# Expert rounds of 96 and 64 slots in turn, constants in two loads, and the filling of the row buffer moved

## The reference

```python
def moe_ffn(h, router, w_gu, w_down):
    logits = (h @ router).astype(jnp.float32)
    top_v, top_i = lax.top_k(logits, TOP_K)          # TOP_K = 2 of N_EXPERTS = 8
    w = jax.nn.softmax(top_v, axis=-1)
    combine = jnp.sum(jax.nn.one_hot(top_i, N_EXPERTS, dtype=jnp.float32) * w[..., None], axis=-2)
    gu = jnp.einsum('btd,edf->btef', h, w_gu)        # w_gu: 8 x 1024 x 2816
    g, u = jnp.split(gu, 2, axis=-1)
    act = jax.nn.silu(g) * u * combine[..., None].astype(h.dtype)
    return jnp.einsum('btef,efd->btd', act, w_down)  # w_down: 8 x 1408 x 1024
```

## Time and profile before

| | us |
|---|---|
| median of 3 runs (2498.81 to 2507.88) | 2501.84 |
| the profiled execution's own time | 2506.24 |
| its span in the profile | 2504.4 |
| PE busy | 2345.0 (94%) |
| the seven 96-slot rounds of layer 1, from 808.09 | 7 x 52.53 |
| the seven of layer 3, from 2047.40 | 7 x 52.53 |

### The profile page before, as it was taken

How to read it: one execution, slowest core, us unless ns; L and a number is a source line. 1 busy time by engine, 2 the same in 40 slices (tenths; PEclk the granted TensorE clock), 3 DMA queues, 4 the chain that set the end, 5 groups by cost and what they waited for, 6 DMA issues and landing times.

```text
span 2504.4 us, 47903 instructions
## 1 busy us (share of the span) xinstructions
PE 2345.0 (94%) x21465; PEld 1684.2 (67%) x21465; DVE 478.7 (19%) x1359; ACT 401.4 (16%) x843; POOL 67.2 (3%) x111
## 2 busy tenths in 40 slices
PE   5999998999999999999799899999989899999997
PEld 3776667888888544555476588888878675455454
DVE  1234332000113100000021410003345340000001
ACT  1133223000101000000112310002243310000000
POOL 5000000000000000000000000000000000000000
PEclk8999999999998999999999899999999989999998
DMA  9867886653363898999465695323420079899971
GB/s 329 286 235 270 306 314 199 188 156 102 101 202 126 315 345 309 338 346 330 166 194 193 213 278 164 113 67 104 156 78 11 12 279 332 312 344 348 345 264 42
DMA packets 356876, 551.67 MB, mean 220 GB/s; under 512 B 11393, under 2 KB 311937, under 8 KB 344241
## 3 DMA queue, kind: packets, MB, share of 16 engines
q1 hardware_dynamic: 344208, 525.30, 60.6%
q0 software_dynamic: 5840, 17.72, 2.6%
q10 hardware_dynamic: 6688, 6.57, 0.8%
HBM read 537.24 MB, written 16.37 MB: 221 GB/s over the span
## 4 chain that ended last, share of the span: by engine, by line
PE 88%; DVE 4%; ACT 3%; DMA 3%; issue 1%; ACTq 0%; POOL 0%; SPq 0%; POOLq 0%; DVEq 0%
PE ps L632 86%; ACT ring L1334 1%; DMA ring<-in_dn_w_in 1%; ACT work L1334 1%; DMA ring<-in_ada_w 1%; PE ps L1129 1%; DVE ring L1866 0%; DVE ring L1848 0%; DMA work<-y_rows,work 0%; DVE ring L1871 0%; DVE work L1708 0%; DVE ring L1856 0%; PE ps L1022 0%; DMA y_rows<-work 0%; DMA work<-in_x_sample 0%
## 5 line engine op out<-in xcount | busy, mean ns | idle before, releaser
L632 PE MATMUL ps<-ring,work 128*32 128x256 f32 (+5 forms) x9576 | 783.6, 429 | 35.7 <-ACT work L1334 27.9
L632 PE MATMUL ps<-hT,ring 128*128 128x256 f32 x3200 | 711.8, 381 | 5.2 <-DMA ring<-in_dn_w_in 2.8
L632 PEld LDWEIGHTS ps<-hT,ring 128*128 128x128 f32 x3200 | 607.3, 191 | 114.5 <-issue 12.1
L632 PEld LDWEIGHTS ps<-ring,work 128*32 128x32 f32 (+2 forms) x9576 | 394.9, 114 | 402.8 <-issue 242.8
L1334 ACT ACTIVATE work<-ps 128x256 f32<-128x256 f32 (+4 forms) x268 | 110.3, 428 | 1438.7 <-PE ps L632 1243.5
L632 PE MATMUL ps<-work,ring 128*128 128x256 f32 (+1 forms) x1344 | 291.0, 376 | 10.7 <-DVE work L1933 6.2
L632 PEld LDWEIGHTS ps<-work,ring 128*128 128x128 f32 (+1 forms) x1344 | 243.9, 189 | 48.1 <-DVE work L1933 8.4
L632 PE MATMUL ps<-ring 64*64 64x64 f32 (+1 forms) x4192 | 182.4, 229 | 18.1 <-ACT ring L1334 7.2
L632 PEld LDWEIGHTS ps<-ring 64*64 64x64 f32 x4192 | 160.0, 138 | 57.0 <-ACT ring L1334 24.2
L1334 ACT ACTIVATE ring<-ps 128x512 f32<-128x512 f32 (+3 forms) x208 | 101.7, 492 | 342.4 <-PE ps L632 331.3
L632 PE MATMUL ps<-ring,csil 128*2 128x512 f32 x768 | 99.9, 608 | 10.9 <-DMA ring<-in_ada_w 10.7
(11 more groups left out here) (252 smaller groups left out, 985.6 us busy)
## 6 DMA issues: line engine op xcount, KB each, us to landing
ring<-in_moe_w_gu SPq DMA_DIRECT2D x96, 1536.0 KB, 10.0
ring<-in_ada_w SPq DMA_DIRECT2D x96, 1024.0 KB, 7.3
ring<-in_moe_w_down SPq DMA_DIRECT2D x48, 1536.0 KB, 11.5
ring<-in_ff_w_gu SPq DMA_DIRECT2D x88, 512.0 KB, 6.0
ring<-in_dn_w_in SPq DMA_DIRECT2D x32, 1024.0 KB, 5.5
ring<-in_moe_w_gu SPq DMA_DIRECT2D x32, 1024.0 KB, 5.5
ring<-in_ff_w_down SPq DMA_DIRECT2D x44, 512.0 KB, 7.2
ring<-in_moe_w_down SPq DMA_DIRECT2D x32, 512.0 KB, 6.3
```

Source lines behind the costliest of these rows:

```text
L632: return pe.matmul(out, lhsT, rhs, start=start, stop=stop, **kw)
```

## The change

The seven rounds of up to 96 slots become rounds of 96 and 64 in turn. DVE ranks experts 1 to 7 by their picks: the three smallest go to rounds 1, 3 and 5 with 64 slots, the next three to rounds 2, 4 and 6 with 96, the largest to round 7 with 128. Expert 0 stays in round 0 with 96. In a 64-slot round the four column groups hold the 64 tokens twice, against two different parts of the weights. The constants are loaded in two parts, the second in front of the first panel. The filling of `y_rows` goes behind DeltaNet's state stores, and the position table waits for the first panel to be used.

```diff
-CAP, BLK, GW, DW = 96, 32, 384, 256
+CAP, SMALL_CAP, BLK, GW, DW = 96, 64, 32, 384, 256
+ROUND_CAP = [CAP, SMALL_CAP, CAP, SMALL_CAP, CAP, SMALL_CAP, CAP] + [P] * (1 + EXTRA + 1)
...
         @block.sync
-            sp.dma_start(cst[:], a["consts"]).then_inc(consts_in, 16)
+            sp.dma_start(cst[:, 0:C_TF], a["consts"][:, 0:C_TF]).then_inc(consts_in, 16)
...
                 for name, i in sequence(l):
+                    if (l, name, i) == (0, "in", 0):
+                        sp.dma_start(cst[:, C_TF:NCONST], a["consts"][:, C_TF:NCONST]).then_inc(consts_in, 16)
...
                                 sp.wait_ge(moe["p_gu"], (done[0] + r) * 6 + GU_FREE[j])
+                                if j in (GATE_D, UP_D):
+                                    sp.wait_ge(moe["p_dn"], (done[0] + r) * 4 + 1)
...
         @block.gpsimd
-            for x in range(RND):
-                r0 = CAP if x < NARROW else 0
-                po.dma_start(y_rows[P * x + r0:P * (x + 1), :], a["x_prompt"][0, r0:P]).then_inc(filled, 16)
...
+            po.wait_ge(unit_done, PLAN.first[0]["in"][0] + 1)
             po.memset(rpb_sb[0:48, :], 0.0).then_inc(o_z, 1)
...
             dn_states(0)
+            for x in range(RND):
+                r0 = ROUND_CAP[x] if x < NARROW else 0
+                po.dma_start(y_rows[P * x + r0:P * (x + 1), :], a["x_prompt"][0, r0:P]).then_inc(filled, 16)
...
         @block.tensor
             def deltanet(l):
                 i = DN_LAYERS.index(l)
+                pe.wait_ge(consts_in, 32)
...
+                def columns_small(q, pieces, bank, done):
+                    for j, _ in pieces:
+                        landed(q, j)
+                    for k in range(KC):
+                        for x, (j, width) in enumerate(pieces):
+                            for b in range(2):
+                                t = 2 * x + b
+                                ins = mm(ps[BLK * t:BLK * (t + 1), bank, 0:width], xg[:, k, BLK * b:BLK * (b + 1)],
+                                         weights(j, width)[:, k, :], k == 0, k == KC - 1)
+                    ins.then_inc(moe["p_gu"], done)
...
+                def down_small(q, s):
+                    pe.wait_ge(moe["a_at"], q * 3 + (1 + 2 * s))
...
+                    for c in (range(6, 11) if s else range(6)):
+                        w, n = down_rows(c), c - 6 * s
+                        for b in range(2):
+                            at = P * (n % 3) + 64 * (n // 3) + BLK * b
+                            for x in range(2):
+                                t = 2 * x + b
+                                ins = mm(ps[BLK * t:BLK * (t + 1), 4 + x, :], ma_T[:, s, at:at + BLK],
+                                         w[:, 512 * x:512 * x + 512], c == 0, c == 10, skip_group_check=True)
+                        if c in (2, 4, 7, 10):
+                            ins.then_inc(moe["p_dn"], 1)
+
+                def small(q):
+                    pe.wait_ge(moe["a_xg"], q + (i + 1))
+                    pe.wait_ge(moe["d_xg"], q + (i + 1))
+                    columns_small(q, ((GATE[0], GW), (GATE[1], GW)), PG[0], 1)
+                    columns_small(q, ((UP[0], GW), (UP[1], GW)), PU[0], 3)
+                    columns_small(q, ((GATE[2], GW), (GATE_D, DW)), PG[1], 1)
+                    columns_small(q, ((UP[2], GW), (UP_D, DW)), PU[1], 1)
+                    turn_small(q, 0)
+                    down_small(q, 0)
+                    pe.wait_ge(moe["d_act"], q * 3 + 3)
+                    pe.wait_ge(moe["d_g"], q + (i + 2))
+                    gather(0)
+                    gather(1)
+                    turn_small(q, 1)
+                    down_small(q, 1)
...
                 body(q0, True)
-                with pe.Fori(1, NARROW) as r:
-                    body(q0 + r, False)
+                with pe.Fori(1, NARROW, 2) as r:
+                    small(q0 + r)
+                    body(q0 + r + 1, False)
...
         @block.vector
             def overflow(l):
                 link(stt(taken[:, 0:NE], count, float(NE), es, ALU.mult, ALU.subtract))
-                link(dve.tensor_reduce(top_e, taken[:, 1:NE], AX.X, ALU.max))
-                link(ts(is_top, taken[:, 0:NE], top_e, None, ALU.is_equal))
...
+                link(tt(before_e[:, 0, :, 1:NE], taken[:, 0:NE, None].to_broadcast([P, NE, NARROW]),
+                        taken[:, None, 1:NE].to_broadcast([P, NE, NARROW]), ALU.is_gt))
+                link(dve.tensor_reduce(rank, before_e[:, 0, :, 1:NE], AX.X, ALU.add))
+                ts(high[:, 0], rank, 2.5, None, ALU.is_gt)
+                ts(high[:, 1], rank, 5.5, None, ALU.is_gt)
+                link(ts(where[:, 0:NE], rank, 2.0, 1.0, ALU.mult, ALU.add))
+                link(stt(where[:, 0:NE], high[:, 0], -5.0, where[:, 0:NE], ALU.mult, ALU.add))
+                link(tt(where[:, 0:NE], where[:, 0:NE], high[:, 1], ALU.subtract))
...
```

More of the change, by code:

```diff
@@ new lines, in turn_small @@
+                def turn_small(q, s):
+                    pe.wait_ge(moe["d_act"], q * 3 + (1 + 2 * s))
+                    if s == 1:
+                        pe.wait_ge(moe["a_at"], q * 3 + 1)
+                    for c in range(2 if s else 3):
+                        ins = pe.transpose(ps[:, 6, c * P:(c + 1) * P], ma_s[:, s, c * P:(c + 1) * P], ident)
+                    if s == 1:
+                        ins = pe.transpose(ps[:, 6, 2 * P:2 * P + 64], ma_s[0:64, s, 2 * P:3 * P], ident[0:64, 0:64])
+                    ins.then_inc(moe["p_tr"], 1 + s)
@@ new lines, in down_small @@
+                def down_small(q, s):
+                    pe.wait_ge(moe["a_at"], q * 3 + (1 + 2 * s))
+                    if s == 0:
+                        pe.wait_ge(moe["a_y"], q)
+                        pe.wait_ge(moe["d_y"], q)
+                        for j in (8, 9):
+                            landed(q, j)
+                    else:
+                        landed(q, 10)
+                    for c in (range(6, 11) if s else range(6)):
[8 more added lines that the diff above has]
+                            ins.then_inc(moe["p_dn"], 1)
@@ L1555, in store, with output_small, store_small, small @@
                             .then_inc(moe["y_out"], 16)
+                def output_small(q):
+                    act.wait_ge(moe["p_dn"], q * 4 + 4)
+                    act.wait_ge(moe["y_out"], q * 64 + 64)
+                    f(y_m[0:64, :], ps[0:64, 4, :], ACT.Copy).then_inc(moe["a_y"], 1)
+                def store_small(q, r):
+                    act.wait_ge(moe["a_y"], q + 1)
+                    act.wait_ge(moe["d_y"], q + 1)
+                    for x in range(4):
+                        act.dma_start(y_rows[bass.ds(r * P, 64), QUARTER * x:QUARTER * (x + 1)],
+                                      y_m[64 * (x // 2):64 * (x // 2) + 64, QUARTER * (x % 2):QUARTER * (x % 2 + 1)]) \
+                            .then_inc(moe["y_out"], 16)
+                def small(r):
+                    q = q0 + r
+                    output(q - 1)
+                    act.wait_ge(moe["p_gu"], q * 6 + 1)
+                    act.wait_ge(moe["d_act"], q * 3)
+                    f(mg_s, ps[:, PG[0], 0:GW], ACT.Silu).then_inc(moe["a_silu"], 1)
+                    store(q - 1, r - 1)
+                    act.wait_ge(moe["p_gu"], q * 6 + 5)
+                    act.wait_ge(moe["d_act"], q * 3 + 1)
+                    f(mg_s[0:64, DW:GW], ps[0:64, PG[1], DW:GW], ACT.Silu)
+                    f(mg_s[:, 0:DW], ps[:, PG[1], 0:DW], ACT.Silu).then_inc(moe["a_silu"], 2)
+                    act.wait_ge(moe["p_tr"], q * 3 + 1)
+                    act.wait_ge(moe["p_dn"], q * 4)
+                    f(ma_T[:, 0, :], ps[:, 6, 0:GW], ACT.Copy).then_inc(moe["a_at"], 1)
+                    tokens(q + 1)
+                    act.wait_ge(moe["p_tr"], q * 3 + 3)
+                    f(ma_T[:, 1, 0:2 * P + 64], ps[:, 6, 0:2 * P + 64], ACT.Copy).then_inc(moe["a_at"], 2)
                 def body(r, first):
@@ L1610, in experts @@
                 body(0, True)
-                with act.Fori(1, NARROW) as r:
-                    body(r, False)
+                with act.Fori(1, NARROW, 2) as r:
+                    small(r)
+                    body(r + 1, False)
                 output(q0 + NARROW - 1)
@@ L2059, in overflow @@
                 link(stt(taken[:, 0:NE], count, float(NE), es, ALU.mult, ALU.subtract))
-                link(dve.tensor_reduce(top_e, taken[:, 1:NE], AX.X, ALU.max))
-                link(ts(is_top, taken[:, 0:NE], top_e, None, ALU.is_equal))
[L2062 to L2070, removed]
+                link(tt(before_e[:, 0, :, 1:NE], taken[:, 0:NE, None].to_broadcast([P, NE, NARROW]),
[6 more added lines that the diff above has]
+                link(tt(where[:, 0:NE], where[:, 0:NE], high[:, 1], ALU.subtract))
+                link(tt(cap_e, high[:, 0], high[:, 1], ALU.add))
+                link(ts(cap_e, cap_e, float(CAP - SMALL_CAP), float(SMALL_CAP), ALU.mult, ALU.add))
```

(27 more changed lines are left out.)

26 lines of the change are left out of this document (14 added, 12 removed).

## The result

The changed kernel takes 2438.26 us (median of 4 runs, 2434.91 to 2439.59), the kernel before 2504.86 in runs beside it: ratio 0.9725 [0.97, 0.975], 66.6 us less. I had forecast 2395, a range of 2384 to 2422. The sign is right, and 40 us of the forecast gain of 107 are missing; the other 3 of the 43 between 2438 and 2395 come from the kernel before, whose median was 2501.84 when I forecast and 2504.86 here. The profiled execution took 2439.59.

The account below looks back on a forecast made before the run. Expert rounds bound by TensorE with DMA close behind, prologue by transfers. Small rounds 97.8 less waits 4.8 gives 93, plus prologue 14, is 107 us off the median 2501.84: 2395, range 2384 to 2422.

Parts of the forecast that it names:

- two limits: Expert rounds: 52.53 us of TensorE for a 96-slot round, and a DMA time of 46.2 us a round.
- Small rounds: 64-slot expert rounds: 16.3 us less each, 36.2 us a round; three in each of two layers save 97.8 us.
- Rival 3: Down part of 64-slot rounds: 512-column groups not side by side, gain 50, 2452 us; chance 0.07 with other small-round faults.
- Waits for weights: Expert rounds: TensorE waits 2.4 us a layer in front of round 6, 4.8 in both, none in round 4.
- D: Transfer time of one expert round's weights and stores without a gap: 46.2 us; each us more costs 4.45 a layer.
- the margin of 1.5 us: In front of round 4: weights land at 176 us from round 0's start, TensorE needs them at 177.5, no wait.
- rival 1: Expert rounds: transfers limit earlier, with D 49.4 and a wait of 16.6 us a layer, 2423 us; chance 0.20.
- Prologue: Before the first panels: tokens and `ada_w` units land earlier, first panel at 39.7, panel waits go; 14 us saved.
- The fills and the table: Moved `y_rows` fills and position table: priced at 0; 3 us if fills delay output panels, 5 if the ring is emptier.
- rival 4: Expert rounds: a ranked expert overflows its slots, adding a 128-slot round of 64.5 us; one in each layer 2524; chance 0.03.

Follow-up runs that it names:

- experiment 1: Changed kernel with TensorE's rounds 1 to 6 written out one behind the other instead of a loop run three times: 2411.26 us, ratio 0.9611.
- experiment 3: Kernel before with the prologue part of the change alone (constants in two loads, position table and fills moved): 2493.94 us, ratio 0.9944.
- experiment 4: Changed kernel with the old prologue, so the rounds of 96 and 64 slots alone: 2449.71 us, ratio 0.976.
- experiment 7: Changed kernel with TensorE's rounds 1 to 6 written out, and half of each expert's weights loaded in rounds 1 to 7: 2394.22 us, ratio 0.9565.

## Why the prediction missed

**The step that failed** is "So there are two limits: 52.53 us of TensorE, and a DMA time". There is a third, the fetch of PE's own instructions, which stands in the sum at nothing and cost 39.3 us at four jumps. The diff showed it: two rounds written out in a loop that had held one. The count of instructions for each pass was at hand, and I read the order of the work and not its length. The trace of before had a hint as well. The queue `q8 instruction` carried 10 packets of 16 KB in the seven rounds of layer 1 (829.93 to 1197) and none in rounds 2 and 3 (935 to 1040), so the loop ran from what PE held. In the changed kernel, view of the transfers in the same stretch (packets, MB, share):

```profile
q8 instruction: 35, 0.57, 0.6%
```

That is 25 packets or 0.41 MB more. The three passes of the loop take 9, 11 and 11 packets, where before the first pass took 6 and the other five none. Written out, the same rounds take about as many (31 packets from 815 to 1197 in experiment 1), and they cost nothing. So what costs is not the volume, it is that after a jump back the instructions have not been fetched ahead: the packet starts only 2.4 to 2.6 us into the gap, and PE goes on when it has landed. The rows show the packets and the waits; that PE holds a fixed amount of code is argued from them.

**Small rounds.** Forecast 36.2 us, measured 36.3 and 36.4. The sum of 97.8 becomes 6 x 16.1 = 97. Right, and by the stated parts: four matmuls of 512 columns run side by side. Rival 3 is out.

**Waits for weights.** Forecast 4.8 us, in front of round 6 alone. In the changed kernel there are none, since the idle places give the transfers time. With those gone it is 15.4 us, in front of rounds 4 and 6. D was nearly right: pairs that are bound by transfers take 93.0 to 93.8, half of which is 46.5 to 46.9, forecast 46.2. At the forecast's 4.45 for each us of D, that is worth 1.3 to 3.1 us a layer, of the 4.0 (layer 1) and 6.5 (layer 3) that the forecast wait of 2.4 falls short by. The rest is the margin of 1.5 us in front of round 4, where the unit landed 179.9 us after the start of round 0 (792.93) and not 176: I let transfers arrive at an even rate, but the unit that the 96-slot round needs first comes free 11.7 us before that round, needs 12 us to land behind a full queue, and SP is 1.7 to 3.6 us late with it. So rival 1 held in a small degree, and with the fetch solved it would have given about 2395 + 10.6 = 2406, near the 2411 and 2412 measured.

The Trainium skill's 358 GB/s ("DMA: Bandwidth & Descriptors", "Where 436 GB/s comes from"), by which D would have been 49.3, does not hold here: the windows above carry 381 and 383 GB/s over 89 us.

**Prologue.** Forecast 14 us. The seventh unit started at 29.00 (forecast 28.2), the eighth at 32.50 (31.0), the first panel at 41.39 (39.7), the third at 64.37 (about 62). It is 13.8 by the spans of experiment 3, 11.4 between experiment 4 and the full change, 11.1 at the dense layer. Right, with up to 3 us too much; the first panel is 1.7 late, of which 1.5 stand already at the eighth unit. Experiment 3, with the same prologue, has the first panel at 40.34, so about 1 us is spread. The fills and the table cost nothing that can be seen. Some 3 us that were gained before layer 1's end are lost in layers 2 and 3 ahead of the experts (36.0 us earlier after layer 1, 33.1 at the start of layer 3's); that was not followed up.

**The extra round** (rival 4) did not come: one 128-slot round a layer.

**The account.** 97 for small rounds - 39.3 at the jumps back + 11 to 12 for the prologue - 3 lost in layers 2 and 3, whose place is not known, = 66 to 67; measured 66.6. Seen from the forecast: 107, less the 39.3, plus the 4.8 of waits for weights that did not come, less some 6 for the prologue, layers 2 and 3 and 0.8 of the small rounds. So part of one error hid another.

## What to carry to other kernels

When a change makes the body of a loop longer, count the instructions of one pass on each engine and look in the trace of before whether the loop fetches instructions while it runs; here 349 matmuls a pass were free, and 399 paid at three jumps of five. Where a loop passes that edge and runs only a few times, writing it out cost nothing on the engine (all periods 88.93 us in experiment 7) and beat both kernels (0.9611 and 0.9627 of the kernel before, about 26 us under the changed one); if it must stay a loop, put its jump where the engine waits for something else. An idle place of one kind hides waits of another: solve the first and look again before pricing the second.

## What was not expected of the hardware

- A jump back over 399 or more float32 matmuls, not over 349, leaves PE idle for 5 to 9 us, then at a granted clock of 0.50 to 0.66 until about 952 at the first one (39.3 us for four jumps, of which 29.4 idle).
- The first gap depends little on the traffic and the second a lot: 5.3 + 3.7 to 3.9 us where the DMA share is 0.95 in the window 860 to 920, 4.3 to 4.5 + 1.0 to 1.2 where it is 0.56.
- A second gap of 3.7 to 3.9 us comes after four or five more records in layer 1 and not in layer 3. In both layers the next packet starts 5.9 us after the first (945.55 behind 939.68, 2164.36 behind 2158.47); in layer 3 PE has work until then (20 records). That would fit a loop whose start lies close to the end of a packet in layer 1, which is argued and was not tried. Why with 399 matmuls some jumps are free stays open. Whether ACT, DVE or SP have an edge of the same kind wasn't tried.
